# The dense parts' first unit computed from the unnormalised residual, with raw steps interleaved, squares added in pairs, and the down weights' split moved

## What is computed

```python
def rms_norm(x, gain):
    xf = x.astype(jnp.float32)
    y = xf * lax.rsqrt(jnp.mean(xf * xf, axis=-1, keepdims=True) + EPS)
    return (y * gain.astype(jnp.float32)).astype(x.dtype)

def swiglu(x, w_in, w_out):
    gate, up = jnp.split(x @ w_in, 2, axis=-1)
    return (jax.nn.silu(gate) * up) @ w_out

# in second_block, for each of the 2 layers (mod comes from c, w_ada, b_ada)
hn = rms_norm(h, g_ffn1[l]) * (1.0 + sc1) + sh1
h = h + 0.5 * (1.0 + gt1) * swiglu(hn, w_ffn1_in[l], w_ffn1_out[l])
...
hn = rms_norm(h, g_ffn2[l]) * (1.0 + sc3) + sh3
h = h + 0.5 * (1.0 + gt3) * swiglu(hn, w_ffn2_in[l], w_ffn2_out[l])
```

## Time and profile before

| | us |
|---|---|
| runs of the kernel before | 1924.10, 1930.51, 1935.44 (median 1930.51) |
| the profiled execution, its time | 1928.03 |
| its span, first to last instruction | 1926.2 |
| mean granted TensorE clock | 0.992 of full speed |
| busy: TensorE, VectorE, ScalarE, GpSimd | 1864.3, 1161.8, 784.9, 31.1 |

### The profile page before, as it was taken

How to read it: one execution, slowest core, us unless ns; L and a number is a source line. 1 busy time by engine, 2 the same in 40 slices (tenths; PEclk the granted TensorE clock), 3 DMA queues, 4 the chain that set the end, 5 groups by cost and what they waited for, 6 DMA issues and landing times.

```text
span 1926.2 us, 30151 instructions
## 1 busy us (share of the span) xinstructions
PE 1864.3 (97%) x12550; PEld 1678.8 (87%) x12550; DVE 1161.8 (60%) x1766; ACT 784.9 (41%) x1099; POOL 31.1 (2%) x63
## 2 busy tenths in 40 slices
PE   8999989899999999999999999999999999999998
PEld 7788969778866667999988889999999998879998
DVE  1495355566666655877647548776876547545552
ACT  3223543444444444444443234444443444334342
POOL 6000000000000000000000000000000000000000
PEclk9999999999999999999999999999999999999999
DMA  9344511556799987787541057776776441034441
GB/s 265 108 145 140 163 57 45 208 187 245 272 395 374 397 323 295 283 319 294 173 142 37 23 195 271 304 305 266 268 304 254 153 153 45 23 131 159 173 175 64
DMA packets 124567, 391.58 MB, mean 203 GB/s; under 512 B 11802, under 2 KB 72516, under 8 KB 95120
## 3 DMA queue, kind: packets, MB, share of 16 engines
q1 hardware_dynamic: 122192, 387.71, 54.2%
q0 software_dynamic: 1936, 0.89, 0.2%
q10 hardware_dynamic: 304, 1.06, 0.1%
HBM read 388.58 MB, written 1.05 MB: 202 GB/s over the span
## 4 chain that ended last, share of the span: by engine, by line
PE 87%; DVE 6%; ACT 3%; issue 2%; DMA 1%; DVEq 0%; SPq 0%; ACTq 0%
PE bank L547 85%; PE bank L588 1%; DMA slab<-in_w_up 1%; ACT w_hi L1508 1%; DMA slab<-in_w_ffn_in 1%; DVE slab_low L1969 0%; DVE tiny L2014 0%; DVE region L1982 0%; ACT rsB L1431 0%; DVE region L2033 0%; DVE region L2551 0%; DVE region L2528 0%; DVE region L2549 0%; ACT L1395 0%; DVE region L2013 0%
## 5 line engine op out<-in xcount | busy, mean ns | idle before, releaser
L1969 DVE TENSOR_TENSOR slab_low<-slab,w_hi 128x2048 fp32r<-128x2048 f32 x152 | 348.1, 2291 | 203.4 <-ACT w_hi L1508 203.1
L547 PE MATMUL bank<-h_hi,w_hi 128*128 128x256 f32 x1408 | 395.9, 281 | 1.5 <-DVE h_lo L1961 1.5
L547 PE MATMUL bank<-h_lo,w_hi 128*128 128x256 f32 x1408 | 395.3, 281 | 0.0
L547 PE MATMUL bank<-h_hi,slab_low 128*128 128x256 f32 x1408 | 393.8, 280 | 0.0
L1508 ACT ACTIVATE w_hi<-slab 128x2048 fp32r<-128x2048 f32 x152 | 290.8, 1914 | 153.6 <-DMA slab<-in_w_up 76.9
L547 PEld LDWEIGHTS bank<-h_hi,w_hi 128*128 128x128 f32 x1408 | 264.8, 188 | 3.0 <-issue 3.0
L547 PEld LDWEIGHTS bank<-h_hi,slab_low 128*128 128x128 f32 x1408 | 266.0, 189 | 0.0
L547 PEld LDWEIGHTS bank<-h_lo,w_hi 128*128 128x128 f32 x1408 | 265.4, 189 | 0.0
L547 PE MATMUL bank<-gT_hi,d_hi 128*128 128x256 f32 x832 | 234.1, 281 | 0.8 <-DVE gT_lo L2166 0.8
L547 PE MATMUL bank<-gT_hi,d_low 128*128 128x256 f32 x832 | 234.0, 281 | 0.0
L547 PE MATMUL bank<-gT_lo,d_hi 128*128 128x256 f32 x832 | 234.0, 281 | 0.0
(11 more groups left out here) (323 smaller groups left out, 2899.2 us busy)
## 6 DMA issues: line engine op xcount, KB each, us to landing
slab<-in_w_ffn_in SPq DMA_DIRECT2D x88, 1024.0 KB, 8.5
slab<-in_w_up SPq DMA_DIRECT2D x64, 1024.0 KB, 9.1
region<-in_w_ada SPq DMA_DIRECT2D x112, 512.0 KB, 6.6
region<-in_w_ffn_out SPq DMA_DIRECT2D x44, 1024.0 KB, 5.0
region<-in_w_down SPq DMA_DIRECT2D x32, 1024.0 KB, 5.4
slab<-in_w_in SPq DMA_DIRECT2D x23, 1024.0 KB, 5.3
slab<-in_w_mix_in SPq DMA_DIRECT2D x20, 1024.0 KB, 10.1
hT<-in_w_ada SPq DMA_DIRECT2D x32, 512.0 KB, 6.0
```

Of the source, the lines that this page charges most:

```text
L547: return nc.tensor.matmul(o, lhsT, rhs, start=start, stop=True, skip_group_check=True)
L1969: V_.tensor_tensor(slab_low[slot][:, :], slab[slot][:, :], w_hi[h % 3][:, :].bitcast(F), ALU.subtract)\
```

## The change

- The first unit of each dense part is computed from the residual times the gain, without the norm. Its high part (`raw_hi`, ScalarE) and low part (`raw_lo`, VectorE) are made as each residual chunk is ready, in between the residual's additions. The shift stands beside the tokens as two more columns, so a raw product has 258 columns. Gate and up blocks of both steps go to four banks of their own (`raw_place`). Chunks 0 to 3 go to both steps in turn, then chunks 4 to 7 to the first and 4 to 7 to the second.
- The sum of squares stands behind chunk 5 of the first step. VectorE first adds squares 4 to 7 to 0 to 3, so the sum has 4 products instead of 8. The six warming matmuls ahead of the dense parts go.
- `raw_hidden` multiplies the raw gate and up blocks by the norm's factor and adds the shift's product, with SiLU in place between.
- Step 2 takes the normalised chunks as they come, into bank 4. Step 3 waits for the first raw step's hidden values, and the first down for step 2's.
- The fourth slab's high part stands in the middle of ScalarE's splitting of the normalised chunks; its low part ahead of `raw_hidden`. The down weights of the first unit are split behind it and ahead of the fifth slab.
- In the last slot, the hidden values' high and low parts stand ahead of the table load and of the slab for the next part.
- adaLN pieces are spread over slots 3 to 20. In segment 2 their first load waits for the joint's squares.
- `modulation` and a small `raw_shift` stand ahead of the last copy of the mixture's output and of the residual's additions; some buffers move.

The diff, cut to its core:

```diff
@@ ada_slot
-    return [p for p in range(n) if 1 + p // rate == r]
+    return [p for p in range(n) if (3 + 18 * p // n if seg else 1 + p // rate) == r]
@@ place
-            return bank[s % (2 if unit_of(s).seg == 0 else 4)]
+            seg = unit_of(s).seg
+            if seg and s == SLOTS_OF[seg][0][2] + 2:
+                return bank[4]
+            return bank[s % (2 if seg == 0 else 4)]
+        def raw_place(s0, x, ab):
+            return bank[(s0 + ((0, 3), (1, 2))[x][ab]) % 4][:, 0:T + 2]
@@ TensorE
+            def raw_mm(unit, x, s0, kc):
+                h = unit.halves[x]
+                if kc == 0:
+                    pe.wait_ge(S["ulo_ready"], h + 1)
...
+                for ab in range(2):
+                    o, cols = raw_place(s0, x, ab), slice(ab * P, (ab + 1) * P)
+                    mm(o, hi[:, cols], raw_hi[:, kc, :], kc == 0)
+                    mm(o, hi[:, cols], raw_lo[:, kc, :])
+                    m = mm(o, lo[:, cols], raw_hi[:, kc, :])
+                return m
+            def raw_norm_sum(seg):
+                while len(ring) % RING != 6:
+                    ring.append((None, 0))
+                ps = product("act")
+                pe.wait_ge(S["sq_sum"], seg)
+                for j in range(4):
+                    m = mm(ps[:, 0:T], C("ones"), sq[:, j, :], j == 0)
+                m.then_inc(S["for_act"], 1)
@@ TensorE, ffn
-                for unit, j, s, pending in SLOTS_OF[seg][:-1]:
+                slabs_of(members[0])
+                pe.wait_ge(S["raw_split"], w("raw_split"))
+                for kc in range(KD // 2):
+                    pe.wait_ge(S["raw_split"], w("raw_split"))
+                    for x in range(2):
+                        raw_mm(members[0], x, s0, kc)
+                for x in range(2):
+                    for kc in range(KD // 2, KD):
+                        if x == 0:
+                            pe.wait_ge(S["raw_split"], w("raw_split"))
+                        m = raw_mm(members[0], x, s0, kc)
+                        if kc == KD - 1:
+                            m.then_inc(S["up_done"], 1)
+                        if x == 0 and kc == 5:
+                            raw_norm_sum(seg)
+                for unit, j, s, pending in SLOTS_OF[seg][2:-1]:
                     if j == 0:
                         slabs_of(unit)
-                    if s == s0:
-                        for kc in range(KD):
-                            pe.wait_ge(S["h_split"], w("h_split"))
-                            for x in range(2):
-                                m = ffn_mm(unit, x, s + x, kc)
...
+                    if s == s0 + 3:
+                        pe.wait_ge(S["gut"], s0 + 1)
                     bank_free(s, seg)
                     for kc in range(KD):
+                        if s == s0 + 2:
+                            pe.wait_ge(S["h_split"], w("h_split"))
                         m = ffn_mm(unit, j, s, kc)
...
+                    if s == s0 + 3:
+                        pe.wait_ge(S["gut"], s0 + 3)
+                        ring_free(6)
                     if j:
                         down(UNITS[unit.u - 1])
@@ TensorE, ahead of each dense part
-                norm_sum()
-                keep_warm(6)
@@ ScalarE
-            def split_h(h_hi=h_hi, shift=None):
+            def split_h(h_hi=h_hi, shift=None, src=hT, between=None):
                 for j in range(KD):
+                    if j == 5 and between is not None:
+                        up_high(between)
                     act.wait_ge(S["hn"], w("hn"))
...
+            def raw_norm(seg, gain, shift):
+                tables(LNEXP)
+                act.wait_ge(S["mod_ready"], seg)
+                nc.scalar.activation(raw_hi[:, :, T:T + 2], twice(shift), ACT.Copy).then_inc(S["raw_high"], 1)
+                for d in range(KD):
+                    act.wait_ge(S["x_ready"], w("x_ready"))
+                    nc.scalar.activation(raw_hi[:, d, 0:T], xT[:, d, :], ACT.Copy, scale=gain[:, d:d + 1])\
+                        .then_inc(S["raw_high"], 1)
+                for x in range(0, KD, 2):
+                    nc.scalar.activation(sq[:, x:x + 2, :], xT[:, x:x + 2, :], ACT.Square).then_inc(S["raw_sq"], 1)
+                rsqrt_of(take()[:, 0:T], rsB[:, T:2 * T], 1.0 / D, C("small", 0, 1), "rs")
+                split_h(shift=lambda j: shift[:, j:j + 1], src=sq,
+                        between=next(u for u in UNITS if u.seg == seg).halves[0] + 3)
@@ ScalarE, ffn
+                    if unit is None:
+                        for x in pending:
+                            hidden_high(x)
                         tables(LNEXP)
+                        pending = []
+                    if r == 2:
+                        for x in pending:
+                            hidden_high(x)
+                        down_high(members[0])
+                        up_high(ahead[1])
+                        continue
@@ VectorE
+            def raw_shift(shift):
+                dve.wait_ge(S["raw_high"], w("raw_high"))
+                V_.tensor_tensor(raw_lo[:, :, T:T + 2], twice(shift), raw_hi[:, :, T:T + 2].bitcast(F),
+                                 ALU.subtract).then_inc(S["raw_split"], 1)
+            def raw_low(d, gain):
+                dve.wait_ge(S["raw_high"], w("raw_high"))
+                V_.scalar_tensor_tensor(raw_lo[:, d, 0:T], xT[:, d, :], gain[:, d:d + 1],
+                                        raw_hi[:, d, 0:T].bitcast(F), ALU.mult, ALU.subtract)\
+                    .then_inc(S["raw_split"], 1)
+            def raw_squares():
+                dve.wait_ge(S["raw_sq"], w("raw_sq", KD // 2))
+                V_.tensor_tensor(sq[:, 0:4, :], sq[:, 0:4, :], sq[:, 4:8, :], ALU.add).then_inc(S["sq_sum"], 1)
@@ VectorE, end of moe
                 up_low(members[-1].halves[1] + 3)
+                modulation(0, (0,))
+                raw_shift(ada[:, 0:8])
                 copy_y(N_GROUP - 1)
-                add_output(0, None, "scattered", N_GROUP - 1)
+                add_output(0, None, "scattered", N_GROUP - 1, modg[:, 0, :])
+                raw_squares()
@@ VectorE, ffn
+                def raw_hidden():
+                    rs = rsB[:, T:2 * T]
+                    for x in range(2):
+                        dve.wait_ge(S["up_done"], s0 + x + 1)
+                        for ab in range(2):
+                            step(V_.tensor_copy(shift_col(x, ab), raw_place(s0, x, ab)[:, T:T + 1]))
+                        later()
+                        V_.tensor_tensor(raw_gu[x][0], raw_place(s0, x, 0)[:, 0:T], rs, ALU.mult)\
+                            .then_inc(S["raw_gate"], 1)
+                        step(V_.tensor_tensor(raw_gu[x][1], raw_place(s0, x, 1)[:, 0:T], rs, ALU.mult))
+                    later()
+                    for x in range(2):
+                        dve.wait_ge(S["silu_ready"], s0 + x + 1)
+                        V_.scalar_tensor_tensor(gu_f[x], raw_gu[x][1], shift_col(x, 1), raw_gu[x][0],
+                                                ALU.add, ALU.mult).then_inc(S["gut"], 1)
...
+                    if r == 2:
+                        up_low(ahead[0])
+                        raw_hidden()
+                        for x in pending:
+                            hidden_low(x)
+                        down_low(members[0])
+                        up_low(ahead[1])
+                        continue
@@ VectorE, ahead of ffn2
-                residual(gate(1))
-                norm_dense(gain(2), shift(2))
+                raw_shift(ada[:, 72 * l + 48:72 * l + 56])
+                residual(gate(1), modg[:, l * 6 + 2, :])
+                raw_squares()
+                norm_dense(modg[:, l * 6 + 2, :], ada[:, 72 * l + 48:72 * l + 56])
@@ SyncE, ada_loads
+                        if p == 0 and unit.seg == 2:
+                            sp.wait_ge(S["sq_sum"], unit.seg)
```

More of the change, by code:

```diff
@@ L122 @@
     "h_high": "the high part of a chunk of the normalised residual",
+    "raw_high": "the high part of a shift, or of a chunk of the scaled residual", "raw_sq": "two chunks of its squares",
     "in_high": "the high part of the first norm's output, then of a chunk of the gated sum",
@@ L127 @@
     "h_split": "both parts of a chunk of the normalised residual",
+    "raw_split": "both parts of a shift, or of a chunk of the scaled residual", "mod_ready": "a part's gain and shift",
+    "sq_sum": "its squares, added to four chunks", "raw_gate": "the gate half of a step of the scaled residual, normalised",
     "in_split": "both parts of the first norm's output, then of a chunk of the gated sum",
@@ L1617, in ffn @@
                         hidden_high(x)
-                    for h in ahead[1:]:
-                        up_high(h)
                     if unit is not None and j == 0 and unit is not members[0]:
@@ L1879, in _ @@
                     up_high(h)
-                norm(glu_next=True, shift=shift(2))
```

(16 more changed lines are left out.)

64 lines of the change are left out of this document (41 added, 23 removed).

## The result

The kernel after took 1936.93 us (median of 7 runs, 1934.62 to 1945.19), the kernel before 1927.75 beside it (7 runs). The ratio is 1.0046, with a 95% interval of 1.0027 to 1.0064. So it is slower by some 8.9 us. That is just inside the 0.5% that the prediction called no change, though the interval reaches beyond it, and the time is inside the range of 1926 to 1944. The profiled execution took 1936.93 us, 8.9 more than the one of before (1928.03). The sum of the prediction had said +4.2.

A forecast was written before the change was run, and what follows sets the result against it. TensorE was taken as the bound, with the change decided at four joints. Their sum, +4.2 us, gave 1932.2 for the profiled execution; with 2.5 for the median, 1934.7, called 1934.5 us, range 1926 to 1944.

The forecast's parts named there:

- T: Moment VectorE starts scaling for the norm at a joint, put at R + 9.99 us.
- VectorE's queue behind T: Slab and weight splits at each joint delay hidden values: new TensorE stalls of 3.3 us before step 3, 1.9 before down.
- R: Start of a joint's first raw product; J2 1140.4, J3 about 1333.3, J4 1723.65; first down products end at R + 35.15.
- J1: First joint, from the mixture of experts into a dense part: claimed to cost +1.4 us.
- J2: Second of four joints where a dense part begins: claimed to cost +1.45 us.
- J3: Third joint where a dense part begins: claimed -0.1 us, an old TensorE wait of 0.79 being removed.
- J4: Fourth joint where a dense part begins: claimed to cost +1.5 us.
- rival (b): TensorE's clock stays low through step 3 after the first stall: 15 us more, 1949; chance 0.13.
- SyncE's queue: Fourth unit's slab loads wait for the first adaLN piece until about 782, come some 6 us later; costed at nothing.
- The moved buffers change no time: Term for the buffers the change places elsewhere: claimed no change in time.
- (a): Rival: the stalls at the joints don't come, gain 16.5 us in all, 1914; chance 0.12.
- (c): Rival: first raw product waits or 258 columns cost more, R moves under 3 us, 16 us or more slower; chance 0.07.

The follow-up runs named there:

- experiment 3: Kernel after, with all eight first-raw-step chunks first, the sum later, the fourth slab's splits ahead of the norm's factor: 1927.14 us, 0.9993 to the kernel before.
- experiment 8: Kernel after, with five warming products of constants ahead of step 3's wait: 1936.77 us, ratio 1.0048 to the kernel before.
- experiment 2: Kernel after, with the fifth slab's split a slot later, behind step 2's hidden values: 1937.83 us, ratio 1.0039 to the kernel before.
- 12: Kernel after, with the fifth slab's split a slot later and five warming products ahead of step 3's wait: 1927.77 us in one run.
- experiment 9: Kernel after, with `tiny` 200 columns instead of 184, so hidden values and weight region stand 64 bytes apart modulo 128: 1926.46 us, ratio 0.9984 to before.
- Experiment 1: Kernel before, with only the moved buffers (hidden values and weight region lie where they do after): 1934.58 us, ratio 1.0033 to the kernel before.
- Experiment 4: Kernel after, with the fourth slab's splits ahead of the norm's factor and the fifth's behind step 2's hidden values: 1922.47 us, 0.9965 to the kernel before.
- experiment 11: Kernel of Experiment 4 with `tiny` 200 columns, plus normalised values and adaLN places 64 bytes on in the region: 1914.2 us, 0.9919 to the kernel before.

## Why the prediction was right, and where it was wrong

**Right: the chain behind T.** The step "VectorE's queue behind T" named the length of both waits and who releases them. The first was said as 3.3 us and is 2.9 from start to start (2.6 idle); experiment 3 took the slab out of that queue and the wait went. The second, said as 1.9, is 1.59 once the clock is kept up (experiment 8). The times from R of T, step 3, down start and down end were right to 0.35 us. Small sizes were off: the raw hidden values took 2.0 us to the first fused addition's start and 2.4 to its end, not 2.6; the slab inside the norm and the 258 columns cost what was said, to 0.2 us.

**Right: R, and what the joints add.** J1 was said at +1.4 and is +0.8, J2 +1.45 against +1.2, J3 -0.1 against -0.4, J4 +1.5 against +1.0. All four are too high by the same 0.3, because the old stretch was 28.37 us, not the 28.2 of 240 x 0.1174, and the new one 35.05, not 35.15; at J1 and J4 R was earlier than said by another 0.3 and 0.2. At J1 the order of raw shift and copy does delay the scatter (idle 1.60 in place of 0.78). At J3 the wait of 0.79 for the last down products is gone, as said.

**Right: rival (b) priced the clock.** "If the low level lasts 3 us again, step 3 loses 1.5 us, and the second stall of 1.9 hides it" is what happened: experiment 8 shows the hiding, 2 and 12 the 1.5 us once the cover is gone. By the rule of the Trainium skill, page "TensorE: Matmul & The Clock Gate", section on HAM oscillation, each joint is slow once. That held at all four in the kernel after (0.50 to 0.54 in the 3 us behind the wait at J2 to J4; at J1 the low stretch lies across two windows). In experiment 2 the wait of J1, and in experiment 9 that of J3, left the clock at 1.00; where the rule and these windows differ, the windows decide. The waits that the page describes are longer than these of 2.6 us, so it neither promises nor excludes a low clock here.

**Right, with a wrong time: SyncE's queue.** It was said that the slabs of the fourth unit wait for the first piece's place until about 782. The queue after:

```profile
753.59 35.23 SPq L2854 DMA_DIRECT2D region<-in_w_ada  x5
788.86 1.60 SPq L2812 DMA_DIRECT2D slab<-in_w_ffn_in  x2
```

They came out at 788.86, 7 us later than I had it, and TensorE still has no wait on a slab in the dense parts. The cost of nothing held, with less cover than claimed.

**Wrong: "The moved buffers change no time".** That was costed at nothing with no row behind it and no bound from either side. Experiment 1 prices it at +6.4 us (1.0033, from 1.0019 to 1.0048), more than all four joints. With it the sum would have been 4.2 + 6.4 = 10.6 against 8.9 measured; without it, the joints' 2.6 stand against 4.2. The measured time stayed in the range because the width given to the joints happened to hold what this term brought. That is luck, and so is part of how near the time came: 1934.5 was added up from the median of the three runs shown, 1930.51, and the seven runs have it at 1927.75, so 2.8 us of the missing term were made up by the starting point.

**Not the cause: rivals (a) and (c).** The waits came, and R moved by 5.5 to 5.9 us at J1, J2 and J4.

Why the change as a whole brought nothing: it moved the first product 5.5 to 5.9 us forward (7.1 at J3), as it was meant to, and then let VectorE's slab and weight splits, once hidden under 96 normalised products, stand in line ahead of what TensorE needs, and it moved buffers to where the down products are slower. Experiment 4 keeps the early start and puts the slabs where TensorE doesn't wait: 0.9965.

## What to carry to other kernels

When work is started earlier, follow the queue of the engine that feeds the next step, instruction by instruction: here the win of 5.5 us a joint was given back to the splits of two slabs and of the down weights, and moving the two slabs brought the ratio from 1.0046 to 0.9965. The low clock behind the first wait cost only what the second didn't cover, so here warming paid after that wait was gone, not before. And when a change moves buffers, time the old kernel with the new addresses first: eight floats of padding were worth 0.46% here, about as much as the change lost. A place of one copy in one pair of profiles does not tell that: it moved by 4.5 us between two kernels of equal addresses.

## What the runs showed that was not expected

- A down product (256 columns, fp32r) starts each 113.6, 118.1 or 119.9 ns with its two tiles 64, 32 or 0 bytes apart modulo 128, in six layouts at full clock; 48 of them took 5.46, 5.68 and 5.76 us. It is no rule for every product: experiment 11 has 117.7 at a distance of 64, and the up products `h_hi,w_hi` have 117.8 to 119.8 at a distance of 0. Why is not known.
- The same wait of 2.5 to 2.6 us left the granted clock at 1.00 at two joints (experiment 2, J1; experiment 9, J3; step 3 took 5.64 and 5.69 us from its first to its last product) and brought the low level at the ten others of these two kernels and the kernel after (7.15 to 7.21 us). What decides between them the runs don't show.
